# Reordering page chunks, bias products, a key patch and sample scores around a decoder's compression and attention

## The reference

```python
def compress_blocks(rows, pe, w1, w2):      # rows: past tokens of the pages, keys or values
    z = rows.reshape(b, l // BLOCK, BLOCK, g, d) + pe[None, None, :, None, :]
    z = jnp.transpose(z, (0, 1, 3, 2, 4)).reshape(b, l // BLOCK, g, BLOCK * d)
    return jax.nn.silu(z @ w1) @ w2
...
# compressed branch: scores of all blocks, softmax, choice of 16 blocks
# selected branch: softmax over the 16 chosen blocks; window branch: over the last 512 tokens
# each score gets a bias that depends on the distance of query and key; gates merge the branches
```

## Time and profile before

| what | value |
|---|---|
| median of three runs | 1634.8 us (1633.76 to 1637.62) |
| profiled execution | 1641.61 us |
| its span, first to last instruction | 1639.9 us |
| compression in it | from about 142.8 to 237.5 us |
| attention in it | from about 238 to 433 us |

### The profile page before, as it was taken

One profiled execution on the slowest core, in us unless ns is written; L12 is line 12 of the kernel. 1 busy time (PEld: TensorE's weight loads), 2 busy tenths in 40 slices (PEclk: granted clock), 3 DMA queues, 4 the chain that ended last, 5 costly groups with the idle time before them and its releaser, 6 DMA issues. The chain is left out here.

```text
span 1639.9 us, 38792 instructions
## 1 busy us (share of the span) xinstructions
PE 1561.1 (95%) x15766; PEld 1461.5 (89%) x15766; DVE 814.5 (50%) x1357; ACT 561.1 (34%) x1061; POOL 566.6 (35%) x509
## 2 busy tenths in 40 slices
PE   7999889999899999999998989999899999999996
PEld 7999866666799999999997879999799999999995
DVE  4333047776555444442267567776646444343145
ACT  4111035666543222222245323334444222222242
POOL 0001317777334343442034334442034344342012
PEclk9999899999999999999999989999899999999998
DMA  5977969877421222233342424342231222233242
GB/s 198 324 257 240 328 250 394 280 248 251 173 91 52 91 90 90 90 104 107 106 160 80 117 66 133 102 156 91 69 126 39 90 90 90 90 100 118 90 159 88
DMA packets 89281, 238.39 MB, mean 145 GB/s; under 512 B 18509, under 2 KB 21247, under 8 KB 87825
## 3 DMA queue, kind: packets, MB, share of 16 engines
q1 hardware_dynamic: 83832, 222.72, 40.5%
q0 software_dynamic: 2992, 9.71, 1.7%
q10 hardware_dynamic: 2314, 3.96, 0.7%
HBM read 217.81 MB, written 23.77 MB: 147 GB/s over the span
## 5 line engine op out<-in xcount | busy, mean ns | idle before, releaser
L875 DVE TENSOR_TENSOR layer_w_lo<-ring,layer_w_hi 128x1024 fp32r<-128x1024 f32 (+1 forms) x136 | 223.1, 1641 | 257.9 <-ACT layer_w_hi L754 257.9
L1033 PE MATMUL layer_ps<-layer_x_hi,layer_w_hi 128*128 128x260 f32 x1312 | 268.6, 284 | 3.8 <-DVE layer_w_lo L875 2.7
L1033 PE MATMUL layer_ps<-layer_x_hi,layer_w_lo 128*128 128x260 f32 x1312 | 267.7, 284 | 0.0
L1033 PE MATMUL layer_ps<-layer_x_lo,layer_w_hi 128*128 128x260 f32 x1312 | 267.2, 283 | 0.0
L754 ACT ACTIVATE layer_w_hi<-ring 128x1024 fp32r<-128x1024 f32 (+1 forms) x136 | 158.7, 1168 | 206.8 <-PE layer_ps L1033 206.8
L1033 PE MATMUL layer_ps<-layer_h_lo,layer_w_hi 128*128 128x260 f32 x960 | 217.4, 287 | 8.8 <-DVE layer_h_lo L884 8.8
L1033 PEld LDWEIGHTS layer_ps<-layer_x_hi,layer_w_hi 128*128 128x128 f32 x1312 | 204.1, 189 | 5.4 <-DVE layer_w_lo L875 2.9
L1033 PEld LDWEIGHTS layer_ps<-layer_x_hi,layer_w_lo 128*128 128x128 f32 x1312 | 204.1, 189 | 0.0
L1033 PEld LDWEIGHTS layer_ps<-layer_x_lo,layer_w_hi 128*128 128x128 f32 x1312 | 203.5, 189 | 0.1
L1033 PE MATMUL layer_ps<-layer_h_hi,layer_w_hi 128*128 128x260 f32 x704 | 172.8, 286 | 4.8 <-DVE layer_w_lo L875 4.8
L1033 PE MATMUL layer_ps<-layer_h_hi,layer_w_lo 128*128 128x260 f32 x704 | 170.2, 282 | 0.0
(11 more groups left out here) (345 smaller groups left out, 2893.7 us busy)
## 6 DMA issues: line engine op xcount, KB each, us to landing
ring<-in_w_gu SPq DMA_DIRECT2D x88, 512.0 KB, 3.4
ring<-in_w_down SPq DMA_DIRECT2D x48, 704.0 KB, 4.1
ring<-in_hgrn_w_in SPq DMA_DIRECT2D x32, 512.0 KB, 5.9
arena<-in_cache_cmp SPq DMA_DIRECT2D x59, 256.0 KB, 5.8
ring<-in_nsa_w_in SPq DMA_DIRECT2D x21, 512.0 KB, 5.2
kv_slot<-in_slc_kv SPq DMA_DIRECT2D x32, 256.0 KB, 4.2
arena<-in_slc_kv SPq DMA_DIRECT2D x32, 256.0 KB, 4.6
X<-in_slc_kv SPq DMA_DIRECT2D x32, 256.0 KB, 4.1
```

What stands on the lines that cost most here:

```text
L875: dve.tensor_tensor(self.w_lo[slot][:, 0:kcs * P], c.ring[:, s, 0:kcs * P], self.w_hi[slot][:, 0:kcs * P].bitcast(F32), ALU.subtract).then ...
L1033: mm = pe.matmul(bank[:, h, 0:TH], wt[slot][:, a], xt[:, x, COLS[h]], start=start and part == 0, stop=stop and part == 2)
```

## The change

It has four parts. In `CHUNKS` the entries 6 and 7 change places, so the ring chunk of 11 pages comes ahead of the key bank's of 16, in the lists of SP, POOL and PE; what PE did after chunks 6, 7, 8 now follows chunks 7, 8, 9. The last two `far` products go behind the last chunk on PE, and their copies behind the silu on ACT. DVE does `patch_window` as attention's first instruction. `sample_scores` goes inside `mix`, right behind the sample's values where there are any, at those `p` whose second step carries no bank.

```diff
-CHUNKS = ((0, 16), (1, 16), (2, 11), (3, 11), (0, 10), (1, 16), (3, 16), (2, 11), (0, 11), (1, 10))
+CHUNKS = ((0, 16), (1, 16), (2, 11), (3, 11), (0, 10), (1, 16), (2, 11), (3, 16), (0, 11), (1, 10))
...
             chunk(6)
+            chunk(7)
             block_scores()
...
             turn_scores()
-            chunk(7)
+            chunk(8)
...
-            chunk(8)
+            chunk(9)
             far(4)
             far(5)
-            chunk(9)
             pe.wait_ge(hidden, 3)
...
-            for j in range(4, 6):
-                far(j)
             for s in range(4):
                 act.wait_ge(chunk_done[s], taken(s, NCH - 1))
             silu_pages(1)
+            for j in range(4, 6):
+                far(j)
...
-            def mix(s):
+            def mix(s, between=None):
...
+                if between is not None:
+                    between()
                 v = at.Vtok[:, :, :].rearrange("p j (b n) -> p j b n", b=2)[:, :, br]
...
-                    mix(2 * p - 4)
-                if p in scored_in:
+                first = p in scored_in and 2 * p - 3 not in bank_of
+                if p >= 2:
+                    mix(2 * p - 4, (lambda: sample_scores(scored_in[p], p)) if first else None)
+                elif first:
+                    sample_scores(scored_in[p], p)
+                if p in scored_in and not first:
                     sample_scores(scored_in[p], p)
...
+            patch_window()
             for p in range(PAIRS + 3):
...
                     blocks_first()
-                    patch_window()
```

## The result

The change made the kernel slower: 1640.8 us in the median of 20 runs (1635.35 to 1647.36), against 1635.9 us of the kernel before in the same series. The ratio is 1.0031, 95% interval 1.0019 to 1.0043, so +3 to +7 us. The prediction was 1634.6 us, hardly a change (-0.2 us), with a range up to 1639.0. The kernel became slower and lies outside the range.

What follows compares the result with a forecast made beforehand. PE, busy in 95% of the 1639.9 us span, was taken to bound the kernel. Terms of +0.5 (chunk order), -1.2 (bias products) and +0.5 us (attention) summed to -0.2 us, giving 1634.6 us, range 1629.0 to 1639.0.

Steps and rivals of the forecast that it cites:

- Chunk order: Compression: exchanging ring and key bank's chunks costs +0.5 us, with bounds of -6.8 and +6.4 us.
- The landing: Compression: the last key page lands at 201.5 us, after PE asks for the key pages at 197.1 us.
- The count of bytes: DMA queues: 2.88 MB of ring chunk minus 1.17 MB spare leave 4.4 us, so key pages land at 200.4 us.
- the new stall: Compression: PE waits 4.4 us for the key pages, then their chunk takes 10.1 us, ending at 211.6 us.
- the ring pages only push the key pages back: Rival, compression: key pages land at 207.4 us, +5.7 us in all, 1640.5 us; chance 0.15.
- Bias products: End of compression: the moved far products fall into PE's 2.38 us wait for ACT, -1.2 us; -0.5 us without cover.
- Attention: Attention: key patch first and scores beside values together cost +0.5 us, with bounds of -3.5 and +2.6 us.
- the lead is lost: Attention: PE's lead turns into a longer wait for a page bank, so no gain from the patch is kept.
- the patch's 1.56 us: Start of attention: PE's wait for DVE's key patch, up to 1.56 us, goes, but none is counted as kept.
- The bank of p = 5: Attention: this page bank lands at the same distance from attention's start, so PE waits 2 us or more for it.
- the two later waits: Attention: PE's waits at the two later page banks become longer than 0.6 us.

Runs made afterwards that it cites:

- e3_swap_onehot_late: The changed kernel with SP's load of the 33 one-hot rows moved behind chunk 8's pages; 1635.7 us, ratio 1.0007.
- e4_before_onehot_late: The kernel before with SP's load of the one-hot rows moved behind the ring chunk's pages; 1633.2 us, ratio 0.9987.
- e1_swap_only: The kernel before with the ring and key bank's chunks exchanged and nothing else; 1644.2 us, ratio 1.0053.
- e10_swap_onehot_spread: The changed kernel with the one-hot rows' load cut into 32 rows and 1 row, same place in the queue; 1640.6 us, ratio 1.0037.
- e17_page_rows_33_deep: The changed kernel with one-hot rows late and, in their old place, 33 rows of page memory written into 33 partitions; 1640.5 us, ratio 1.0032.
- e2_no_swap: The changed kernel with the chunk order of before, keeping all other parts; 1634.2 us, ratio 0.9992.
- e15_early_far_share7: The kernel before with one-hot rows ahead of key pages, last two far products behind the last chunk, key pages seven by SP, nine by POOL; 1626.1 us, 0.9962.
- e11_attention_only: The kernel before with the two attention parts alone, key patch first and scores beside values; 1636.9 us, ratio 1.0009.
- e12_before_again: The kernel before, unchanged, run once for a second profile; PE's wait for the key pages was 2.22 us, at full clock.
- e8_onehot_early_far: The kernel before with one-hot rows ahead of the key bank's pages and the last two far products behind the last chunk; 1633.1 us, ratio 0.9987.
- e16_same_rows_128_wide: The changed kernel with one-hot rows late and, in their old place, a same-size stand-in from their memory written into 128 partitions; 1639.0 us, 1.0027.

## Why the prediction was wrong, point by point

**Chunk order, +0.5 us forecast: the step that failed,** at two places.

*The landing.* PE asked for the key pages at 193.19 + 5.02 = 198.2 us (197.1 forecast), and they landed at 204.1, not 201.5. The count of bytes took in both chunks and the spare of 174 to 178 us, which was right, but left out the one-hot rows that the exchange put ahead of the key pages in SP's queue. With the rows out of the way the pages land at 197.8 us (`e3_swap_onehot_late`): then even the count's 200.4 us was too late. That the rows delay the pages by their 33 partitions is shown for the landing, not for the medians. How the loss is shared between the two queues stays open. The rows slow the traffic in the kernel before as well, from 190 to 196 us:

```profile
190.00:196.00 6.00, 2.02 (x38) 1.77 (x34) 0.00 (x0) 0.00 (x0) 2.69 (x6) 0.93 1.04 273
```

Where they come later (`e4_before_onehot_late`) it is 381 to 393 GB/s in this time. But in the kernel before they stand behind the key pages and ahead of the ring pages, and PE has the block scores to do before it needs those. The exchange put them ahead of pages that PE needs right behind a chunk. The Trainium skill ("SBUF — State Buffer", Door 1: The DMA port swizzle) says that partitions 0 to 31 reach only 8 of 16 ports, with 189 GB/s measured for 1 MiB against 328 GB/s with all 128. Those figures are for a transfer by itself; the 286 against 386 GB/s here are rows and pages together, so this case agrees in direction only, and the ports themselves show in no run here.

*What was there to win or lose.* The sum set the new stall against 4.0 + 10.1 us of one execution that was itself 6 us above the median. Wait and chunk together took 11.0 us in the mean of four executions with the old order. With the exchange and a 33-row transfer ahead it was 15.05 (after), 17.37 (`e1_swap_only`), 13.93 (`e10_swap_onehot_spread`: 4.43 + 9.50) and 17.30 us (`e17_page_rows_33_deep`), mean 15.9. By this measure the term is about +4.9 us, where 14.5 - 14.1 = 0.4 us was forecast: of the error some 3 us lie in the size before and 1.4 in the size after. In the changed kernel's own profile the size after nearly came out, 15.05 us against 14.5, by luck: the wait was 1.5 us longer, by the rows left out, and the chunk 1 us shorter.

The measure leaves out later waits; the ring chunk waited 1.85 and 0.69 us in two of the four executions with the old order. Attention's start takes these in. It lies at 238.07, 237.18, 235.90 and 236.13 us in those four, and at 239.15, 241.85, 238.90 and 239.11 us in the other four. With 1.2 us added where the bias products had moved, the means are 237.1 and 240.7 us: +3.5 us. So the term is some +3.5 to +4.9 us, only roughly known from four executions each. The rival that the ring pages only push the key pages back gave nearly this time, 1640.5 us, from a landing at 207.4 us that never came: the right number by another cause.

**Bias products, -1.2 us: right.** PE's wait fell from 2.38 to 1.18 us, and to 1.18 or 1.19 us in `e2_no_swap`, `e3_swap_onehot_late` and `e15_early_far_share7`. ACT's copies, which now follow the silu, begin at 235.60 us and end at 236.29, ahead of PE's last products at 235.78 + 2.08 = 237.9 us.

**Attention, +0.5 us: within its bounds, and rather too small.** The parts alone gave 1.0009 (0.9991 to 1.0026), -1.5 to +4.2 us. From attention's start to the first products of the layer's end (L1033), the ten profiles with its new order have 195.9 to 200.9 us, 197.4 in the mean, and the six with the old order 193.8 to 197.2 us, 195.6 in the mean. That is about +1.7 us, with a wide spread. With it, the term of the exchange and the bias products, the sum is +4.0 to +5.4 us, inside the ratio's +3 to +7. That the lead is lost was right, and its place half so: most of the patch's 1.56 us goes 6 us later already, in the wait for DVE's biases (0.57 us before, 1.94 after, 2.22 in `e11_attention_only`). In the kernel before, this line follows the patch's wait:

```profile
248.08 1.93 PE L1859 MATMUL pa_s<-arena,HT 128*32 128x128 f32 x32 [0.57 <-DVE arena L2105]
```

The bank of p = 5 then comes a fixed time after attention's start, as argued: 283.39 - 238.07 = 45.3 us before, 284.58 - 239.15 = 45.4 after, and 45.1 to 45.8 us in the other executions. The wait of 3.03 us by itself proves nothing, since the kernel before has as long a one in its second profile (`e12_before_again`):

```profile
282.66 1.31 PE L1859 MATMUL pa_s<-kv_slot,HT 128*32 128x128 f32 x32 [2.99 <-DMA kv_slot<-in_slc_kv]
```

Of the two later waits one grew (0.61 to 1.71 us) and one shrank (0.33 to 0.16), against the forecast that both grow; `e12_before_again` has no wait for pages at either. (The two issues of the earlier trace rows are thirteen apart, as the prediction reckons, not fourteen.)

**Where the win of a timely key chunk goes** can be seen in `e3_swap_onehot_late`, which has no stall there and yet is no faster than before. Against the mean of 11.0 us for wait and chunk it wins 3.8 us, and 1.2 us at the bias products. In its one profile it gives back 2.3 us at chunk 9 (6.99 us instead of 4.65), 1.06 us inside chunk 8, 0.9 us at the second group of bias products (2.91 us instead of 1.98), and 1.8 us in attention (196.9 us against 195.1 before).

## What to carry to other kernels

When a transfer is moved ahead of another in a queue, list everything that passes with it, small transfers too, and price each by the rate while it flows, not by its bytes: 0.34 MB into 33 partitions delayed the pages behind it by 6.3 us here. Take the stall that a change removes from several executions; one profile, far from its median, overstated it by 3 us. Where one queue's last page sets a chunk's start, sharing the pages differently between queues can win more than reordering: 0.9962 in `e15_early_far_share7` against 0.9987 in `e8_onehot_early_far`, though not all of that gain is explained.

## What the runs showed of the hardware

A transfer into 33 partitions lowers what all DMA engines move together (286 GB/s in `e17_page_rows_33_deep` against 386 in `e16_same_rows_128_wide`) while they show the same busy share of 1.04, so a full share doesn't mean a full rate.

PE's clock fell in some executions around the second group of `far` products, whose operand has 33 rows, though PE was not idle. In `e12_before_again`, where PE had no gap from 206.86 us on:

```profile
211.00:214.00 3.00, 3.00 (x32) 1.65 (x28) 0.00 (x0) 0.71 (x2) 0.00 (x0) 1.00 1.14 433
214.00:218.00 4.00, 4.00 (x16) 1.64 (x16) 2.55 (x10) 1.60 (x3) 0.00 (x0) 0.64 0.95 389
218.00:224.00 6.00, 6.00 (x112) 6.00 (x110) 0.00 (x0) 0.08 (x1) 0.00 (x0) 0.67 0.13 36
```

Between the levels of 2.4 and 1.2 GHz it averages 0.64 and 0.67 there, and chunk 8 takes 7.25 us instead of 5.07. In the changed kernel's profile the same products run at 1.00. What decides it was not found; it is one source of the difference between executions. Another lies behind attention, where the kernels are the same: from the products of L1033 to the span's end there are 1204.2 us in the changed kernel (1639.4 - 435.19), 1206.7 in the kernel before and 1195.7 in its second profile (1628.8 - 433.07).
